# Moving the weight-sum DMAs of the mixer stage behind the inverse's last level, and their copies ahead to the last w_out chunk

## The reference, cut to what matters

```
proj = rmsnorm(x) @ w_in                     # 1024 x 3608
mix  = [ GLA heads (4), gated DeltaNet heads (4) ]
x    = x + mix @ w_out                       # 1024 x 1024
up   = causal_dwconv(rmsnorm(x) @ w_up)      # 1024 x 5632, width 3
x    = x + (silu(a) * b) @ w_down            # 2816 x 1024
y    = rmsnorm(x)
```

## Time and profile before

| what | value |
|---|---|
| median of three runs | 3168.86 us |
| profiled execution, its own time | 3172.17 us |
| span in the profile | 3170.5 us |
| TensorE matmul busy | 3052.9 us, 96% of the span |
| VectorE, ScalarE, GpSimd busy | 1834.5, 926.6, 328.4 us |
| granted TensorE clock, mean | 0.98 |
| DMA traffic | 530.24 MB |

### The profile page before, as it was taken

One profiled execution on the slowest core, in us unless ns is written; L12 is line 12 of the kernel. 1 busy time (PEld: TensorE's weight loads), 2 busy tenths in 40 slices (PEclk: granted clock), 3 DMA queues, 4 the chain that ended last, 5 costly groups with the idle time before them and its releaser, 6 DMA issues. The chain is left out here.

```text
span 3170.5 us, 55638 instructions
## 1 busy us (share of the span) xinstructions
PE 3052.9 (96%) x21721; PEld 1977.2 (62%) x21721; DVE 1834.5 (58%) x4382; ACT 926.6 (29%) x2026; POOL 328.4 (10%) x609
## 2 busy tenths in 40 slices
PE   8999999999999999999779999989999999999998
PEld 4555556555555655564458888877888884444443
DVE  2566666556666556765566666677776764222223
ACT  2223322323332322333334444433444441000000
POOL 1111111111101111110110000000110110000000
PEclk9999999999999999999679999999999999999999
DMA  7276576676676654622666788775555566322211
GB/s 249 87 196 176 165 204 183 185 195 178 168 206 179 189 132 149 151 83 64 183 217 214 239 246 249 209 247 159 165 175 171 168 233 234 109 66 70 70 64 63
DMA packets 361026, 530.24 MB, mean 167 GB/s; under 512 B 23756, under 2 KB 252404, under 8 KB 350211
## 3 DMA queue, kind: packets, MB, share of 16 engines
q1 hardware_dynamic: 318531, 376.78, 37.0%
q0 software_dynamic: 11072, 86.51, 13.0%
q10 hardware_dynamic: 31168, 63.44, 5.6%
HBM read 473.57 MB, written 203.04 MB: 213 GB/s over the span
## 5 line engine op out<-in xcount | busy, mean ns | idle before, releaser
L758 PE MATMUL mixer_bank<-arena,hnt 128*128 128x451 f32 x2048 | 865.7, 554 | 10.0 <-DMA arena<-in_w_in_dram 8.5
L758 PEld LDWEIGHTS mixer_bank<-arena,hnt 128*128 128x128 f32 x2048 | 366.2, 191 | 300.9 <-issue 294.4
L2367 PE MATMUL mlp_psum<-mlp_room,arena 128*128 128x256 f32 (+1 forms) x1848 | 446.4, 386 | 16.7 <-DVE mlp_room L2764 5.9
L2367 PEld LDWEIGHTS mlp_psum<-mlp_room,arena 128*128 128x128 f32 x1848 | 353.6, 192 | 74.9 <-DMA arena<-s_blk 6.7
L2367 PE MATMUL mlp_psum<-arena,mlp_room 128*128 128x256 f32 (+1 forms) x1320 | 328.1, 387 | 8.1 <-DVE arena L2769 8.1
L2367 PE MATMUL mlp_psum<-arena 128*128 128x256 f32 (+1 forms) x1144 | 282.2, 385 | 5.2 <-PEq L3000 4.8
L2367 PEld LDWEIGHTS mlp_psum<-arena,mlp_room 128*128 128x128 f32 x1320 | 253.6, 192 | 48.2 <-issue 8.5
L792 PE MATMUL mixer_bank<-wo,th 128*128 128x512 f32 x512 | 249.7, 611 | 3.0 <-DMA wo<-in_w_out_dram 2.4
L1218 ACT ACTIVATE proj<-mixer_bank,x_rs 128x451 f32<-128x451 f32 x128 | 81.3, 635 | 575.2 <-PE mixer_bank L758 543.4
L2367 PEld LDWEIGHTS mlp_psum<-arena 128*128 128x128 f32 x1144 | 218.0, 191 | 42.6 <-issue 7.3
L2456 PE MATMUL mlp_psum<-arena,mlp_room 128*128 128x512 f32 x560 | 242.9, 592 | 0.0
(11 more groups left out here) (405 smaller groups left out, 3911.1 us busy)
## 6 DMA issues: line engine op xcount, KB each, us to landing
wo<-in_w_out_dram SPq DMA_DIRECT2D x260, 256.0 KB, 2.9
arena<-q_blk SPq DMA_DIRECT2D x88, 512.0 KB, 4.5
mlp_room<-q_blk SPq DMA_DIRECT2D x66, 512.0 KB, 4.8
arena<-in_w_blk_dram SPq DMA_DIRECT2D x66, 384.0 KB, 3.5
arena<-s_blk SPq DMA_DIRECT2D x66, 384.0 KB, 3.4
q_blk<-s_blk POOLq DMA_DIRECT2D x8, 2816.0 KB, 19.7
t_blk<-in_d_blk_dram POOLq DMA_DIRECT2D x6, 2816.0 KB, 18.2
mlp_room<-act_t SPq DMA_DIRECT2D x28, 512.0 KB, 5.4
```

The lines of the kernel that those rows point to most:

```text
L758: x = pe.matmul(bank[ring(g)][0:N, 0:GW], hnt[:, k, 0:N], w[:, k, g * GW:(g + 1) * GW], start=(k == 0), stop=(k == KT - 1))
L2367: x = pe.matmul(psum[:, bank, 0:N], weights[:, k * C:k * C + C], xb_of[block_of(n)][:, right, k, 0:N], start=(j in (1, 2, 5) and k == 0), ...
```

## The change

It moves when the stash DMAs are issued. Both halves of a sum are issued by POOL after the memset of the inverse's last level (`a == NL - 1`, that is 6). The second half now waits for the landing of the first, and the first for the landing of the sum before. The wait for `s_wo_used` goes from POOL. The copy is issued at ACT right behind the tanh of the convolution (L1340), which in prompt tiles from 1 on already waits for the use of all 16 chunks.

```diff
@@ stash_sum (POOL)
                         if part == 0:
-                            gp.wait_ge(s_wo_used, 16 * t)
                             gp.wait_ge(s_stash_copied, 16 * (n + 1))
-                            if n:
-                                gp.wait_ge(s_stash_added, 32 * n)
+                        if 2 * n + part:
+                            gp.wait_ge(s_stash_added, 16 * (2 * n + part))
@@ mixer (POOL)
                     .then_inc(s_ug_made, 1)
-                stash_sum(t, 0)
...
-                    if a == 2:
+                    if a == NL - 1:
+                        stash_sum(t, 0)
                         stash_sum(t, 1)
@@ mixer (ACT)
                 act.activation(tq[:, :, 0:N], cv[:, :, 0:N], ACT.Tanh, scale=0.5).then_inc(s_conv_tanh, 1)
+                stash_copy(t)
...
                     inverse_rms(0, front)
-                    stash_copy(t)
```

## The result

The changed kernel takes 3250.68 us (median of four runs, 3244.8 to 3259.72) against 3168.74 us (median of four runs of the kernel before, the three of above and one more): 1.0267 times as long, 95% interval 1.0247 to 1.0286. It is slower by 82 us; the forecast was 3275 us. The profiled execution of the changed kernel took 3244.8 us with a span of 3243.1, 72.6 us over the one of before. Behind the line that the change takes out, lines have moved by one or two (L792 is now L791, L993 is L992, L678 is L677).

A forecast was written before the change was run, and what follows sets the result against it. TensorE was taken as the bound, busy 3052.9 of 3170.5 us. The terms summed as 3172.17 + 95 + 28 - 16.6 = 3278.6 us, or 3275 us against the median of runs; range 3205 to 3322 us.

The forecast's parts named there:

- Term 1: Inverse in tiles 1 to 12: late instruction fetches beside bulk DMA vanish, giving back 16.6 us.
- The rule of the Trainium skill against it: Instruction fetch: refills of 16 KiB blocks are mostly hidden, so nothing is given back and the sum is 16.6 us more.
- Term 2: Next tile's start: second half delays xc and chunk 4, so TensorE stands 95 us in all (55 to 120).
- The rule against term 2: Queue sharing at the tile's start: engines drain whole packets of descriptors per ring, so the chunk stops nearly vanish.
- Term 3: TensorE's clock drops to half behind the chunk stops, slowing matmuls: 28 us in all (0 to 45).
- At nothing: Copy's issue at ACT, its waits, POOL's wait for the first half, and the copy beside resid: no cost.
- A: Tile start: halves and chunks on different rings hinder each other less, only the fetch gain remains: 3152 us; chance 0.08.
- B: Fetch stops return elsewhere and the shorter first half lets xc pass: within 9 us of 3169; chance 0.05.
- C: ACT waits at the copy for a late sum, evacuations queue behind, no fetch gain: 3327 us; chance 0.08.
- D: Tile start: collision happens but xc comes first, TensorE stands 4 to 5 us a tile: 3229 us; chance 0.17.

The follow-up runs named there:

- e14: Changed kernel with each half cut to 16 rows, leaving out most of the weight sums: 3151.93 us, ratio 0.9955 against the kernel before.
- e2: Kernel before with only the copy moved behind the tanh, the halves in their old places: 3182.01 us, ratio 1.0045.
- e12: Changed kernel without the second half's wait for the first half's landing: 3252.92 us, ratio 1.0282 against the kernel before.
- e4: Changed kernel with SP's load of xc issued behind the tile's chunk loads: 3228.69 us, ratio 1.0188 against the kernel before.
- e7: Kernel before with only the copy moved, from position 56 to about 74 behind fill(5): 3165.98 us, ratio 0.9995.
- e11: Kernel before with only the second half moved, from position 53 to the last level (74): 3166.82 us, ratio 0.9997.
- e3: Kernel before with the copy moved behind the tanh and the second half to the last level: 3164.33 us, ratio 0.9986.

## Why the prediction was right, point by point

The direction, the mechanism and its place were right. All three terms were there; the sum of 106 us came out at 82 us, because terms 2 and 3 were too large (in the tiles 79.2 + 19.5 - 16.6 = 82.1). That this meets the 82 us of the medians so closely is partly luck: the two profiled executions differ by 72.6 us.

- **Term 1, given back: predicted -16.6, measured -16.6.** The issue stops are 0 in the changed kernel, and e14 runs all tiles at 92.04. The rule of the Trainium skill against it (Runtime: NRT & Kernel Launch, Instruction fetch mechanics: crossing a block is mostly hidden) holds for most of the fetches (tiles 1 to 12 of the kernel before have 92 of 16 KB and eleven "issue" stops) and not for some of those where small matmuls run beside bulk DMA. My reason for the term was wrong: I took tile 13 as "the one without a loss", because no copy is in flight in it. But tile 11 had no copy either and lost 3.9 us, and tiles 9 and 10 had copy and halves and lost nothing. e2's expectation failed on this. The number came out all the same because the changed kernel has neither in the dense part.
- **Term 2, the stops: predicted 95 us, measured 79.2.** S tiles 10.5 predicted, 9.2 in the mean measured; Q 9.7 and 8.4; R 3.6 and 2.1. The stops are 1.3 to 1.5 us shorter: they end 1.1 to 1.3 us earlier than I had, and begin 0.2 later (10.0 instead of 9.84). Two steps of it show in the rows: the R first half took 13.0 us where I had 14.3, and a chunk lands 0.7 us behind xc (position 19.6 against 18.9 in tile 3), where I gave it 1.4. The sharing was as read, 195 to 193. (Of resid I counted 144 packets once and 128 further on; with 128 the start and end of a half are 4.8 us instead of 4.6.)
- **The rule against term 2** (the Trainium skill, DMA: Bandwidth & Descriptors, Queues, rings and completion order: 9 to 17 descriptors from one ring before the switch) would have made it nearly nothing. In the records q1's pieces pass one for one, and xc takes 18.3 us instead of 4.
- **Term 3, the clock: predicted 28 us, measured 19.5** (the part of the 98.7 lost that is not stops; the 4.6 us by which the kernel before was slowed behind its own stops are in term 1's 16.6). I took 2.7 us behind every long stop and 1.7 behind a short one. It was 1.7 to 2.7 behind the eight long ones, 2.3 in the mean and 18.2 in all, and 0.3 behind those of 1.2 to 2.8 us, 1.2 in all where I had 7: in their tiles (4, 6, 8, 11) the granted clock did not fall at all. The term was sized from a single long stop, and the short ones from tile 11 of the kernel before, where the clock did fall, behind a stop of 2.05 us.
- **At nothing:** the copy at its new place (e14) and POOL's wait (e12) cost nothing, as forecast. In the changed kernel TensorE waits for neither ug nor va.
- **The rivals:** A (rings do not hinder each other) falls with the 18.3 us of xc. B falls with the result. C (ACT waits at the copy) did not happen: the S halves land by position 18, and the copies go out at 31 to 43. D named a stop of 4 to 5 us in each tile, with xc landed first, and 3229 us. The changed kernel is not that, since xc takes 18.3 us. e4, where xc comes last and the chunks meet the half alone, measures 3228.69 us, with 5.1 to 7.1 us of stops in eight tiles and 1.2 in one; that it meets D's time is chance.
- **Outside tiles 1 to 14** the two profiled executions differ by another 9.5 us in the other direction (tile 0, tile 15, the sample tile and the MLP). Tile 15, which has no stash DMA in either, is 3.6 us of it: its "issue" stop went from 2.9 to 0.7 us. These stretches vary by some us among all the kernels run here (tile 15 takes 74.4 to 78.2), so I give it no cause.

**What stays open.** Why a fetch stop falls in one tile and not in the next was not settled: neither the length of the pieces nor the number of queues alone decides it (e7, e11). The place in the code seems to count. Of the 16.6 us of the kernel before, 13.3 are lost in tiles 2, 5, 8 and 11, every third one; their late fetches begin at positions 62 to 63 and 69 to 70, and in tile 1 or 4 they begin at 60, 67 and 73. In e7 these tiles have 10.1 of 13.9 us, in e11 15.1 of 19.1 (tile 11 none). No run moved the code to try this, and no run changed the length of the halves' pieces to try the one-for-one sharing. And a layout without any overlap was not found. A half takes 13 to 19 us alone and a copy 17 to 25; the tile has 27 us from the last chunk to the dense part and about 18 from the last level to the next tile.

## What to carry to other kernels

A bulk DMA between HBM tensors is not free because no engine waits for it: ask at every place what small-piece loads it will share the DMA engines with, count their pieces, and remember that everything queued behind them on the same issuing queue waits as well. Look at what an existing wait keeps apart before taking it out; here one on POOL, seemingly for nothing POOL needed, held an accumulate of 2 to 3 MB off the chunk loads, which have some 4 us to spare (chunk 4 lands at 5.8 in tile 13 of the kernel before and is wanted at 9.8). When traffic is moved, sum what it takes alone and compare with the gap it moves to; here it didn't fit, and of the orders tried the best won 0.1%, two changed nothing and the others lost.

## What the runs showed of the hardware that was not expected

- In each of the changed kernel's eight stops of 7.6 to 9.7 us TensorE's granted clock falls to 0.50 and stays there for 6.8 or 10.2 us, of which 2.8 to 5.1 lie behind the stop. In e4's tile 3, with two stops of 3.4 and 1.7 us, it is at 0.50 for 10.2 us too, and 5.7 of them lie behind the second stop: TensorE is busy for 7.74 us of that stretch, in the changed kernel's tile 3 for 2.82. A shorter stop can thus give back less than its length: 31.5 us of waits became 22 us of time.

```profile
359.90:370.10 10.20, 7.74 (x9) 3.02 (x10) 2.15 (x9) 1.64 (x2) 0.00 (x0) 0.50 0.63 184
```

- POOL did not get two of these accumulating halves under way at once: without any semaphore between them the second was issued 12.9 to 17.7 us after the first, each time 0.3 us after the first had landed (e12).
- Two bulk streams side by side don't stretch each other alike. The copy (2-KB pieces) lands after 22.0 us alone, 33.8 beside one half (e3) and 46.9 beside both (e2). The first half (8-KB pieces) lands only 1 to 4 us later in e3, beside the copy, than in the same place of the kernel before.
- A fetch of 16 KB of instructions that ends late holds TensorE until 1.2 to 1.6 us after its end (54 stops in seven runs, under e14).
